# Angle inputs, low-rank gate product and weight unit 2 in the opening of a decoder-block kernel

## The chip, the cores and the metric

The kernel runs on one core of a Trainium2 chip. The metric is the device time of one execution in microseconds. A core has five engines with a queue each: TensorE (PE, matrix products), VectorE (DVE), ScalarE (ACT), GpSimd (POOL) and SyncE (SP), which here issues nearly all DMAs. Each engine runs its program in order; they meet through semaphores.

## What is computed

A decoder block on x of 256 tokens by 1024. Cut to what matters here:

```python
h = rms_norm(x, norm1_gain[l])
proj = h @ w_in[l]
gq, gk, gv, gr, g_low, mq, mk, mv = parts      # widths 256, 256, 512, 512, 16, 512, 512, 512
gate_logit = g_low @ w_gate_up[l] + b_gate[l]  # low rank: 16
log_a = jax.nn.log_sigmoid(gate_logit) / GLA_GATE_TAU
...                                            # gated linear attention on gq, gk, gv, log_a, gr
q_m = rotary(to_heads(mq, MOBA_HEADS), positions)   # ang = positions * inv_freq; cos, sin
k_m = rotary(to_heads(mk, MOBA_HEADS), positions)
...                                            # causal attention, both groups normed
x = x + jnp.concatenate([o_gla, o_moba], axis=-1) @ w_out[l]
h = rms_norm(x, norm2_gain[l])
x = x + (jax.nn.silu(h @ w_ffn_gate[l]) * (h @ w_ffn_up[l])) @ w_ffn_down[l]
return rms_norm(x, final_norm_gain)
```

## The kernel before

All is f32. A large product is made of three f32r products, `hi*hi + hi*lo + lo*hi`: for every weight, ScalarE casts it from `raw` to `w_hi`, and VectorE subtracts, `w_lo = raw - w_hi`; the activations (`aT_hi`, `aT_lo`) are split alike. Weights come as *units* of 128x2048 (1 MB) through three `raw` slots into rings of six for hi and lo. An in-projection unit is half the depth (four chunks of 128) of one block of 512 columns. Units 0 and 1 are special: they are loaded, cast and multiplied as eight *rows* of 128x512 (`load_first`, `split_first`, `first_row`), so that TensorE can begin early. `unit_ready(u)` is TensorE's wait for a unit, `raw_free(u)` SP's wait for a slot.

The order on every engine is written out by hand. TensorE's opening: 14 warm-up products of zeros, the eight transposes of x tile 0 into the PSUM banks `aux` 0 to 3 (chunks 2b and 2b+1 share bank b), three small transposes to bring the norm gains and the frequencies to partitions, two warm-ups, the transposes of x tile 1, two small transposes more (frequencies spread to 128 rows, positions to partitions), the eight rows (`first_row`), the low-rank product (`gate_low`), the transpose of the other gains (`other_gains`), then the units 2 to 11 (`in_unit`), with the attention's products between them; the logits (`logits`) stand in the middle of unit 2.

ScalarE's opening: `take_xT` scales two chunks of x's transpose by the gains out of PSUM into `aT_hi`, in turn with `split_first` of the rows 1 to 7; then the low weights' cast, `split(2)`, two sums of squares for the norm (`sum_squares`), `split(3)`, and `take_block(0)`. VectorE: the gains' copy, two small copies for the angles, row 0 (cast and low part), then per chunk the `aT_lo` and the row's low part; then the angle work (`pos_f`, `ang`, `nearest_turns`, `turns_hi`, `turns_lo`), unit 2's low part (`split(2)`, L1137), four subtractions of multiples of two pi (`take_off`), the copy of the low-rank result (`lowT`, L1199), the other gains, and so on.

The low-rank product before: the 16 columns of low weights stand in 128 stationary columns (four times a hi and a lo part of 16); sixteen f32r matmuls of 256 columns, `aT_hi` and `aT_lo` per chunk, add up in one place of `aux` bank 2; `w_up` has the up weights on the partitions 0 to 31 (hi and lo), zeros elsewhere.

## Time and profile before

| what | value |
|---|---|
| median of 3 runs | 302.25 us (301.93 to 302.3) |
| the profiled execution | 301.75 us |
| its span in the trace | 300.0 us |
| TensorE busy | 292.4 us, 97% of the span |
| VectorE, ScalarE, GpSimd busy | 242.4, 171.6, 19.1 us |
| granted TensorE clock, mean | 0.996 |

The profile is one execution. The span runs from the first to the last recorded instruction; the execution's own time has 1.75 us more around it. Rows name an instruction by engine, line, operation and tiles (written<-read). PE rows are matmuls, PEld the loads of their stationary operand. In the chain of waits each piece is what the next one waited for, so its pieces add up to the span; in a timeline instructions can overlap by their pipelines.

### The profile page before, as it was taken

The numbers are of one execution on the slowest core, as the hardware profiler recorded it, in microseconds if no ns is written. First come the engines' busy times: TensorE is split into PE (matmuls) and PEld (weight loads), VectorE is DVE, ScalarE is ACT, GpSimd is POOL, SyncE is SP. The second block draws the span as 40 slices with busy tenths as digits, with TensorE's granted clock in tenths as the row PEclk, the third lists the DMA queues.
The fourth block names the chain that finished last, engine by engine and source line by source line (L and its number), as shares of the span: only waits on it lengthen the run. The fifth ranks groups of instructions, "written<-read, shape, count | busy, mean of one in ns | idle before, by whom it ended". The sixth has DMA issues, their size and how long they took to land.

```text
span 300.0 us, 4026 instructions
## 1 busy us (share of the span) xinstructions
PE 292.4 (97%) x1373; PEld 243.3 (81%) x1373; DVE 242.4 (81%) x403; ACT 171.6 (57%) x242; POOL 19.1 (6%) x41
## 2 busy tenths in 40 slices
PE   7999999999999999999999999999999999999992
PEld 7788888788898888887888888888888888888881
DVE  1999999977879687988888888889897978787155
ACT  2898999969765897717170808080808080813123
POOL 5050100000021001300000000000000000000011
PEclk9999999999999999999999999999999999999998
DMA  7987836737867121392929292929291929030003
GB/s 235 364 289 266 263 119 251 218 131 264 298 190 227 53 92 70 95 329 90 331 82 336 79 343 69 346 66 352 63 363 47 367 54 366 25 120 0 0 0 140
DMA packets 37318, 55.45 MB, mean 185 GB/s; under 512 B 2950, under 2 KB 26554, under 8 KB 37306
## 3 DMA queue, kind: packets, MB, share of 16 engines
q1 hardware_dynamic: 37140, 55.13, 54.4%
q10 hardware_dynamic: 166, 0.17, 0.2%
q8 instruction: 7, 0.11, 0.2%
q14 instruction: 5, 0.04, 0.0%
HBM read 53.72 MB, written 1.57 MB: 184 GB/s over the span
## 4 chain that ended last, share of the span: by engine, by line
PE 94%; DMA 2%; DVE 1%; issue 1%; POOL 1%; ACT 0%; SPq 0%; POOLq 0%; DVEq 0%
PE acc L508 15%; PE acc L510 15%; PE acc L509 15%; PE aux L508 13%; PE aux L509 13%; PE aux L510 13%; DMA raw<-in_w_in 2%; PE aux L613 1%; PE acc L562 1%; PE acc L565 1%; PE acc L568 1%; PE aux L683 1%; DVE x_sb L1366 1%; PE aux L707 1%; PE aux L665 1%
## 5 line engine op out<-in xcount | busy, mean ns | idle before, releaser
L1137 DVE TENSOR_TENSOR w_lo<-raw,w_hi 128x2048 fp32r<-128x2048 f32 x47 | 105.6, 2286 | 14.5 <-ACT w_hi L877 14.4
L877 ACT CAST w_hi<-raw 128x2048 fp32r<-128x2048 f32 x47 | 87.9, 1908 | 4.4 <-DMA raw<-in_w_ffn_up 2.1
L508 PE MATMUL aux<-w_hi,aT_hi 128*128 128x512 f32 (+1 forms) x180 | 69.8, 388 | 0.0
L509 PE MATMUL aux<-w_lo,aT_hi 128*128 128x512 f32 (+1 forms) x180 | 69.7, 387 | 0.0
L510 PE MATMUL aux<-w_hi,aT_lo 128*128 128x512 f32 (+1 forms) x180 | 69.7, 387 | 0.0
L1432 DVE STREAM_TRANSPOSE reuse_c<-reuse_c 32x128 f32<-32x128 f32 x160 | 48.4, 303 | 2.4
L1080 ACT CAST pT_hi<-reuse_c 128x512 fp32r<-128x512 f32 x10 | 6.2, 621 | 72.9 <-DVE reuse_c L1432 72.9
L508 PE MATMUL acc<-w_hi,aT_hi 128*128 128x512 f32 x118 | 47.1, 399 | 0.0
L510 PE MATMUL acc<-w_hi,aT_lo 128*128 128x512 f32 x118 | 46.1, 390 | 0.0
L509 PE MATMUL acc<-w_lo,aT_hi 128*128 128x512 f32 x118 | 46.0, 390 | 0.0
L508 PEld LDWEIGHTS aux<-w_hi,aT_hi 128*128 128x128 f32 x180 | 33.8, 188 | 6.9
L510 PEld LDWEIGHTS aux<-w_hi,aT_lo 128*128 128x128 f32 x180 | 33.8, 188 | 6.9
L509 PEld LDWEIGHTS aux<-w_lo,aT_hi 128*128 128x128 f32 x180 | 33.8, 188 | 6.8
L508 PE MATMUL acc<-w_hi,pT_hi 128*128 128x512 f32 x80 | 31.3, 392 | 0.0
L510 PE MATMUL acc<-w_hi,pT_lo 128*128 128x512 f32 x80 | 31.2, 390 | 0.0
L509 PE MATMUL acc<-w_lo,pT_hi 128*128 128x512 f32 x80 | 31.2, 389 | 0.0
L510 PEld LDWEIGHTS acc<-w_hi,aT_lo 128*128 128x128 f32 x118 | 22.2, 188 | 4.8
L508 PEld LDWEIGHTS acc<-w_hi,aT_hi 128*128 128x128 f32 x118 | 22.2, 188 | 4.7 <-issue 0.2
L509 PEld LDWEIGHTS acc<-w_lo,aT_hi 128*128 128x128 f32 x118 | 22.2, 188 | 4.4
L1063 ACT ACTIVATE reuse_c<-aux,rstd 128x256 f32<-128x256 f32 x22 | 10.0, 471 | 19.1 <-PE aux L510 17.9
L508 PEld LDWEIGHTS acc<-w_hi,pT_hi 128*128 128x128 f32 x80 | 15.0, 188 | 3.4 <-issue 0.3
L510 PEld LDWEIGHTS acc<-w_hi,pT_lo 128*128 128x128 f32 x80 | 15.0, 188 | 3.2
(203 smaller groups left out, 285.0 us busy)
## 6 DMA issues: line engine op xcount, KB each, us to landing
raw<-in_w_ffn_gate SPq DMA_DIRECT2D x22, 512.0 KB, 4.3
raw<-in_w_ffn_up SPq DMA_DIRECT2D x22, 512.0 KB, 5.4
raw<-in_w_ffn_down SPq DMA_DIRECT2D x22, 512.0 KB, 6.0
raw<-in_w_in SPq DMA_DIRECT2D x20, 512.0 KB, 4.8
raw<-in_w_out SPq DMA_DIRECT2D x8, 512.0 KB, 4.3
raw<-in_w_in SPq DMA_DIRECT2D x8, 256.0 KB, 6.2
x_sb<-in_x SPq DMA_DIRECT2D x2, 512.0 KB, 3.7
m_moves<-reuse_c SPq DMA_DIRECT2D x1, 512.0 KB, 2.7
```

The costliest lines, as they stand in the source:

```text
L508: nc.tensor.matmul(dst, left_hi[:, k, tok], right_hi, start=first, stop=False)
L509: nc.tensor.matmul(dst, left_hi[:, k, tok], right_lo, start=False, stop=False)
L510: return nc.tensor.matmul(dst, left_lo[:, k, tok], right_hi, start=False, stop=last)
L562: nc.tensor.matmul(acc[:, t, :], aT_hi[:, k, toks[t]], right_hi, start=k == 0, stop=False)
L565: nc.tensor.matmul(acc[:, t, :], aT_hi[:, k, toks[t]], right_lo, start=False, stop=False)
L568: last = nc.tensor.matmul(acc[:, t, :], aT_lo[:, k, toks[t]], right_hi, start=False, stop=k == KC - 1)
L613: last = nc.tensor.transpose(aux[:, bank, n * P:(n + 1) * P], src, ident[:, :])
L877: nc.scalar.copy(w_hi[:, slot % RING, :], raw[:, slot % RAW, :]).then_inc(hi_ready, 1)
L1063: nc.scalar.activation(silu_g[:, t, :], aux[:, GATE_UP_BANKS[parity][t], 0:FF], ACT.Silu, scale=rstd[:, 1, t:t + 1]).then_inc(silu_ready, 1)
L1080: nc.scalar.copy(dst, src.rearrange("p (k s) -> p k s", k=2)).then_inc(hiddenT_hi_ready, 1)
L1137: nc.vector.tensor_tensor(w_lo[:, slot % RING, :], raw[:, slot % RAW, :], w_hi[:, slot % RING, :].bitcast(f32), ALU.subtract).then_inc(lo_ ...
L1432: last = nc.vector.transpose(cols[SQUARE * c:SQUARE * (c + 1), :, :, g, :], rows[SQUARE * g:SQUARE * (g + 1), :, :, c, :])
```

## The change

Six things change in the opening; from unit 3 on the order is the same.

1. Positions and frequencies are loaded to the partitions where they are used: positions as 256 single elements, frequencies as one row repeated to 128 partitions, first and second on ScalarE's queue. The three small transposes and two copies that did this go. The norm gains' DMA moves to SP, between the two x tiles.
2. SP issues weight row 0, waits for x tile 0, and then issues the rows 1 to 7.
3. VectorE's angle work up to `turns_lo` stands ahead of row 0 and around the gains' copy.
4. The low-rank product works in f32: POOL multiplies the raw low weights by the gains, ScalarE copies x's transposes unscaled out of PSUM (`copy_xT`, four copies of 128x512), and eight matmuls write four column groups of 32, two chunks to a group. The logits product adds the groups, `w_up` holding four copies.
5. Unit 2 is cast and split in two halves, each with a load semaphore of its own. The order of `lowT` and the subtractions changes.
6. `fill` counts the loads of a `raw` slot, of which unit 2 no longer uses the common semaphore; `take_block(0)` waits for the low-rank product, since its target shares memory with the copies.

```diff
+        low_w = reuse_d[:, 512:512 + KC * SQUARE].rearrange("p (k w n) -> p k w n", k=KC, n=RANK)
+        xT_raw = [half[:, :].rearrange("p (b n) -> p b n", b=2)[:, b, :] for half in (reuse_a, reuse_b) for b in range(2)]
...
             for t in range(T):
                 sp.dma_start(x_sb[:, t, :], x[0, t * P:(t + 1) * P, :]).then_inc(x_loaded[t], 16)
-            for n in range(KC):
+                if t == 0:
+                    sp.dma_start(gain_rows[0:KC, :], norm1_gain.rearrange("l (k p) -> (l k) p", p=P)).then_inc(norm1_loaded, 16)
+            load_first(0)
+            sp.wait_ge(x_loaded[0], 16)
+            for n in range(1, KC):
                 load_first(n)
...
-            for n in range(2):
-                sp.dma_start(w_up[n * RANK:(n + 1) * RANK, :], w_gate_up[0]).then_inc(up_loaded, 16)
+            for n in range(QUADS):
+                sp.dma_start(w_up[n * SQUARE:n * SQUARE + RANK, :], w_gate_up[0]).then_inc(up_loaded, 16)
...
-                pe.wait_ge(xT_hi_ready, KC)
-                pe.wait_ge(xT_lo_ready, KC)
+                pe.wait_ge(low_w_ready, 1)
+                pe.wait_ge(xT_raw_ready, KC // 2)
                 for k in range(KC):
-                    left = w_hi[:, RING - 1, k * P:(k + 1) * P]
-                    nc.tensor.matmul(aux[:, 2, 0:SEQ], left, aT_hi[:, k, :], start=k == 0, stop=False)
-                    last = nc.tensor.matmul(aux[:, 2, 0:SEQ], left, aT_lo[:, k, :], start=False, stop=k == KC - 1)
+                    group = slice(k % QUADS * SQUARE, (k % QUADS + 1) * SQUARE)
+                    last = nc.tensor.matmul(aux[group, 2, 0:SEQ], low_w[:, k, :, :].rearrange("p w n -> p (w n)"),
+                                            xT_raw[k // 2][:, k % 2 * SEQ:(k % 2 + 1) * SEQ], start=k < QUADS, stop=k >= QUADS)
...
-            act.dma_start(gain_rows[0:KC, :], norm1_gain.rearrange("l (k p) -> (l k) p", p=P)).then_inc(norm1_loaded, 16)
-            act.dma_start(freq_row, inv_freq).then_inc(freq_loaded, 16)
-            act.dma_start(pos_i, positions.rearrange("b (t p) -> (b t) p", p=P)).then_inc(pos_loaded, 16)
+            with nc.allow_non_contiguous_dma("one position a partition"):
+                act.dma_start(pos_i, positions.rearrange("b (t p) -> p (b t)", p=P)).then_inc(pos_loaded, 16)
+            act.dma_start(freq, inv_freq.to_broadcast([P, HALF])).then_inc(freq_loaded, 16)
```

VectorE at the start of the program, before, from its first instruction to row 0's low part (`reuse_c` holds the small inputs):

```order
L1161 MEMSET w_lo 128x256
L1163 COPY gains<-acc 128x8
L1166 COPY reuse_c<-acc 64x1
L1168 CAST reuse_c<-reuse_c 2x128
L1156 CAST w_hi<-raw 128x512
L1158 TENSOR_TENSOR w_lo<-raw,w_hi 128x512
```

The same place in the changed kernel (`reuse_e` holds angles and turns, `w_lo` the cast turns):

```order
L1162 MEMSET w_lo 128x256
L1171 CAST pos_f<-reuse_c 128x2
L1175 TENSOR_SCALAR reuse_e<-reuse_c,pos_f 128x64 x2
L1164 TENSOR_SCALAR reuse_e<-reuse_e 128x128
L1165 TENSOR_SCALAR reuse_e<-reuse_e 128x128
L1179 COPY gains<-acc 128x8
L1181 CAST w_lo<-reuse_e 128x128
L1182 TENSOR_TENSOR reuse_e<-reuse_e,w_lo 128x128
L1157 CAST w_hi<-raw 128x512
```

Five angle instructions (L1171 to L1165) now stand ahead of the gains' copy and two behind it, all ahead of row 0's cast.

ScalarE from the last chunks of x to unit 3, before:

```order
L900 ACTIVATE aT_hi<-aux,gains 128x256 x2
L906 CAST w_hi<-raw 128x512 x2
L916 CAST w_hi<-low_raw 128x32x16
L877 CAST w_hi<-raw 128x2048
L883 ACTIVATE reuse_f,ss<-x_sb 128x1024 x2
L877 CAST w_hi<-raw 128x2048
```

The same place in the changed kernel (`reuse_a` and `reuse_b` take the unscaled x):

```order
L892 ACTIVATE aT_hi<-aux,gains 128x256 x2
L905 COPY reuse_a<-aux 128x512
L898 CAST w_hi<-raw 128x512 x2
L905 COPY reuse_a<-aux 128x512
L916 CAST w_hi<-raw 128x1024 x2
L905 COPY reuse_b<-aux 128x512 x2
L875 ACTIVATE reuse_f,ss<-x_sb 128x1024 x2
L869 CAST w_hi<-raw 128x2048
```

The cast of the low weights is gone, four copies have come, and two of them stand behind unit 2's halves.

## Rows read from the trace of the kernel before

**Rows 1.** The page: busy time of the engines, and the chain's shares.

```profile
PE 292.4 (97%) x1373; PEld 243.3 (81%) x1373; DVE 242.4 (81%) x403; ACT 171.6 (57%) x242; POOL 19.1 (6%) x41
...
PE 94%; DMA 2%; DVE 1%; issue 1%; POOL 1%; ACT 0%; SPq 0%; POOLq 0%; DVEq 0%
```

**Rows 2.** Chain of waits, first 10 us: start, length, what.

```profile
0.80 0.38 SPq L336
...
1.71 5.34 DMA raw<-in_w_in
...
7.07 0.44 DVE w_hi L1156
...
7.64 0.70 PE acc L562 x2
...
9.01 0.47 PE acc L568 x2
```

**Rows 3.** Chain of waits, around the low-rank product (16 pieces, L589 and L590).

```profile
19.02 0.12 PE aux L589
...
20.82 0.12 PE aux L590
20.93 0.15 PE aux L577
21.09 0.43 PE acc L508
```

**Rows 4.** Chain of waits: f32 products (logits; attention output; state update).

```profile
24.04 0.86 PE aux L620 x4
...
76.99 1.45 PE aux L683 x13
78.44 0.59 PE aux L695 x8
```

**Rows 5.** Timeline of ScalarE, 12 to 16 us: start, length, instruction, [idle before, releaser].

```profile
12.04 0.86 ACT L900 ACTIVATE aT_hi<-aux,gains 128x256 fp32r<-128x256 f32 x2
12.76 1.16 ACT L906 CAST w_hi<-raw 128x512 fp32r<-128x512 f32 x2
...
15.52 1.91 ACT L877 CAST w_hi<-raw 128x2048 fp32r<-128x2048 f32 x1 [1.07 <-DMA raw<-in_w_in]
```

**Rows 6.** One line's instructions: ScalarE copies of 128x512 from PSUM, min/median/max ns.

```profile
L979 ACT COPY reuse_f<-aux x2: 585/588/591, 69.5 to 70.0; 128x512 f32<-128x512 f32 x2
```

**Rows 7.** DMA issues of the first 8 us: count, size of each, median us to landing.

```profile
x_sb<-in_x SPq DMA_DIRECT2D x2, 512.0 KB, 3.7
...
low_raw<-in_w_in SPq DMA_DIRECT2D x1, 64.0 KB, 6.4
```

**Rows 8.** Timeline of VectorE, 14 to 21 us.

```profile
14.89 1.54 DVE L1158 TENSOR_TENSOR w_lo<-raw,w_hi 128x512 fp32r<-128x512 f32 x1
...
16.61 0.47 DVE L1188 TENSOR_SCALAR reuse_e<-acc,pos_f 128x64 f32<-128x64 f32 x2
...
17.64 0.23 DVE L1191 CAST w_lo<-reuse_e 128x128 fp32r<-128x128 f32 x1
17.90 0.29 DVE L1192 TENSOR_TENSOR reuse_e<-reuse_e,w_lo 128x128 f32<-128x128 f32 x1
18.22 2.29 DVE L1137 TENSOR_TENSOR w_lo<-raw,w_hi 128x2048 fp32r<-128x2048 f32 x1
```

**Rows 9.** Timeline of all engines, first 7 us; ACTq rows are issues.

```profile
1.44 0.23 ACTq L867 DMA_DIRECT2D reuse_c<-in_inv_freq  x1
...
5.36 0.11 PEld L545 LDWEIGHTS acc<-ident,reuse_c 1*64 1x64 f32 x1
...
5.57 0.17 DVE L1163 COPY gains<-acc 128x8 f32<-128x8 f32 x1 [4.38 <-PE acc L542]
...
5.84 0.20 DVE L1168 CAST reuse_c<-reuse_c 2x128 f32<-2x128 int32 x1
6.31 0.84 ACT L900 ACTIVATE aT_hi<-aux,gains 128x256 fp32r<-128x256 f32 x2 [3.04 <-PE aux L534]
```

More of the change, by code:

```diff
@@ L349, in rows_unit @@
                                   w[row + h * half * P:row + (h + 1) * half * P, col:col + width]
-                                  .rearrange("(k p) n -> p k n", p=P)) for h in range(2)])
+                                  .rearrange("(k p) n -> p k n", p=P)) for h in range(2)], sems)
             def gate_up_unit(slot, j, h):
@@ L914, in _ @@
                     take_xT((n + 1, n + 2) if n < KC - 1 else ())
-            act.wait_ge(low_loaded, 16)
-            nc.scalar.copy(low_w[:, :, :, 0, :], low_raw[:, :, :].unsqueeze(2).to_broadcast(LOW_COPIES)).then_inc(low_hi_ready, 1)
-            split(2)
+                if n in (5, KC - 1):
+                    copy_xT((n - 5) // 2)
+            for h in range(2):
+                act.wait_ge(half_loaded[h], 16)
+                half = slice(h * UNIT // 2, (h + 1) * UNIT // 2)
+                nc.scalar.copy(w_hi[:, EARLY, half], raw[:, EARLY, half]).then_inc((half_hi_ready, hi_ready)[h], 1)
+            for pair in range(2, KC // 2):
+                copy_xT(pair)
             for t in range(T):
@@ L1161, in _, with nearest_turns, take_off @@
             nc.vector.memset(warm.bitcast(f32), 0.0).then_inc(warm_built, 1)
+            def nearest_turns():
+                then(nc.vector.tensor_scalar(turns, ang, 1.0 / (2.0 * np.pi), MAGIC, ALU.mult, ALU.add))
+                then(nc.vector.tensor_scalar(turns, turns, -MAGIC, None, ALU.add))
+            def take_off(n, part):
+                then(nc.vector.scalar_tensor_tensor(out=ang, in0=n, scalar=-part, in1=ang, op0=ALU.mult, op1=ALU.add))
+            dve.wait_ge(pos_loaded, 16)
+            nc.vector.tensor_copy(pos_f[:, :], pos_i).then_inc(pos_ready, 1)
+            dve.wait_ge(pos_ready, 1)
+            dve.wait_ge(freq_loaded, 16)
+            for t in range(T):
+                last = nc.vector.tensor_scalar(ang[:, t * HALF:(t + 1) * HALF], freq, pos_f[:, t:t + 1], None, ALU.mult)
+            then(last)
+            nearest_turns()
             dve.wait_ge(gains_in_psum, 1)
```

94 lines of the change are left out of this document (36 added, 58 removed).

## The prediction

> **What bounds the kernel now.** I read the page first: TensorE is busy for 292.4 of 300.0 us, and the chain that ended last is 94% TensorE [rows 1]. So a change pays only where TensorE waits or where it has less to do. Then I read the chain of waits at the two places that the diff touches. At the start the chain runs through the DMA of weight row 0 (issued at 1.71, landed after 5.34 us), VectorE's cast of that row at 7.07, and TensorE's first weight product at 7.64; the third group of products, at 9.01, follows without a hole [rows 2], and from there to the end of the eight rows TensorE is the chain. The second place is the end of the rows: sixteen low-rank products of 0.12 us each from 19.02 to 20.93, then the transpose of the other gains (0.15), and unit 2's first product at 21.09 [rows 3]. Nothing stands between them, so the 1.91 us of the low-rank product are on the path to the last instruction, and what is saved there comes off the whole, provided its new inputs and unit 2 are ready sooner too.
>
> **The low-rank product.** It becomes eight f32 matmuls with 256 moving columns and 32 result partitions, four column groups in turn. The trace shows one f32 matmul as two records: the two logits matmuls, also 256 columns, are four records in 0.86 us, 0.215 each [rows 4]. Sixteen records one behind the other would be 3.44 us. Whether groups run side by side is read from the state update L695: four f32 matmuls of 128 columns, in two column groups of 64, take 0.59 us for eight records, while whole-array matmuls of the same length, L683, take 1.45 for thirteen, 0.1115 each [rows 4]. Eight in a row would be 0.89. In pairs they are 4 x 0.1115 = 0.45, and 0.14 is left over for changing the array's form. So two groups do overlap. With four, sixteen records make four rounds: 4 x 0.215 + 0.14 = 1.00 us. The transpose behind it uses another form, so I charge the 0.14 once more: 1.14. No row shows four groups at once. The bounds are 1.00 (four, one change of form), 1.87 (only pairs: 8 x 0.215 + 0.14 = 1.86) and 3.44 (none); I take 1.14, since the nearest row, L695, has the full overlap that its number of groups allows. Term: 1.14 - 1.91 = **-0.77 us**, with -0.91 and +1.53 as its ends.
>
> The Trainium skill, "TensorE: Matmul & The Clock Gate", Part 3, gives a 2.38-fold speedup for three column tiles, 79% of the ideal; carried to four tiles, an estimate from that page, 3.44 / 3.17 = 1.09 us and a term of -0.82. Its page "TensorEngine Tiling (Array Packing)", Key Properties, says that a change of the tiling mode drains the engine; the 0.14 in L695 agrees.
>
> **What the product now waits for.** TensorE stands at the gate for the scaled weights from POOL and for four copies of the transposed x by ScalarE, and every later matmul is queued behind that wait. ScalarE, from its rows: the chunks 6 and 7 at 12.04 take 0.86 (to 12.90) [rows 5]; the first copy of 128x512 out of PSUM takes 0.59 [rows 6] (13.49), two casts 1.16 (14.65) [rows 5], the second copy 0.59 (15.24). Then unit 2 in halves: the whole cast took 1.91 and had waited for its DMA until 15.52, so both halves are there by 15.52, and the halves end near 16.2 and 17.2. Two more copies: 18.4. TensorE arrives at 19.02, so 0.6 us are spare. If the halves land later by more than that, TensorE waits for the excess. The cast of the low weights leaves ScalarE, which paid for part of the copies. POOL's one operation has half as many elements as the one before and no longer waits for ScalarE; the weights' DMA is issued later on SP but has 6.4 us to landing mostly because of the queue ahead of it [rows 7], which stays the same.
>
> **Unit 2 and VectorE.** Before, the angle steps from 16.61 to 18.22 stood ahead of unit 2's low part, which ran from 18.22 to 20.51 [rows 8], 0.58 ahead of TensorE. Now these steps have moved ahead of row 0, and after the last row (14.89 + 1.54 = 16.43) only two subtractions of 0.32 (spacing as of 17.90 to 18.22) stand before the two halves, 2.29 together: ready at about 19.4. TensorE needs it at 19.02 + 1.14 + 0.15 = 20.3. So the shorter product is not caught by unit 2; without the moved angle work it would have been (20.51 against 20.3). That cover is what the angle move is worth: it gives no time of its own. ScalarE's squares and unit 3 come about 1 us later (18.4 against 15.52 + 1.91 = 17.43 before [rows 5]); I cost that at nothing, since TensorE's share of the chain leaves no room for a wait on the units from 3 on [rows 1], and unit 3 is wanted only after all of unit 2.
>
> **The start.** VectorE now waits for positions and frequencies before it copies the norm gains, and behind that copy are ScalarE's first chunk, VectorE's row 0 and all of TensorE. Its work from the landing F of the frequencies to the cast of row 0: from 16.61 to 17.64 for products and turns (1.03), the gains copy 0.17 [rows 9], then 17.64 to 18.22 for the split of the turns (0.58) [rows 8]: 1.78. Row 0 stands at 7.07, so the work is hidden if F is below 5.29. Before, the frequency row was second on ScalarE's queue (issued at 1.44) and TensorE took it at 5.36, behind other work; positions, third, were taken at 5.84 without a wait for them [rows 9]. Both are upper bounds. The x tiles, 512 KB each, needed 3.7 us from issue [rows 7]; from 1.44 that is F = 5.14, and a small load is hardly slower than a tile. So I take no shift. The loads are more pieces than before, 256 single positions and 128 rows of frequencies, and may push row 0 by some tenths. In the other direction, the seven rows that SP now holds back until x tile 0 has landed (by 0.80 + 3.7 = 4.5) are not in row 0's way; the earliest TensorE could start is with the first chunk, 6.31 + 0.42 = 6.73 instead of 7.64 [rows 2, 9]. Bounds of the start: -0.9 and, without the rival below, +0.5; taken 0. Held-back row 1, issued at 4.5 and landed after 3.7 like a tile in an empty queue, is there at 8.2; its cast takes 0.58 and TensorE wants it at 9.01 + 0.47 = 9.48. Behind the held rows on SP are the low weights, unit 2, the gains, four copies of the up weights (two issues more) and unit 3; the queue of transfers is full throughout, so I cost these at nothing. The small transposes taken off TensorE lie in its wait for row 0 and are worth nothing.
>
> **Sum.** 301.75 us was the profiled execution (span 300.0); 301.75 - 0.77 = 300.98 there. The median of the runs is 302.25, 0.5 above it; on that footing 302.25 - 0.77 = **301.5 us**. A measurement of this kernel can tell about 0.2%, 0.6 us, from no change, so faster means under 301.65.
>
> **Rivals.** (1) *Only pairs overlap.* The product then takes 1.86 and the gain is 0.05: 302.2 us. For it: the trace shows two groups and no more. Against: L695 uses all of its groups. (2) *No overlap with 32-wide groups*, so the change does not do what it says: 3.44, thus +1.53: 303.8 us. Against: both L695's time and its form. (3) *The angle inputs come late*, the one on the slower side: VectorE is stopped at its first instruction of the program's real work, and gains, row 0 and TensorE with it. If the frequencies land like the low weights, which also come in small pieces, after 6.4 us [rows 7], F is 1.44 + 6.4 = 7.84, row 0 is cast at 9.62 instead of 7.07, +2.55, and the whole is +1.78: 304.0 us. It costs from F = 5.29, eats the gain at 6.06 and shows as slower from about 6.66. Between, with F at 5.84 as the positions' bound, +0.55 leaves -0.22: 302.0. For it: the pieces are small and share the engines with 1 MB of x; against: they are issued first. The Trainium skill, "DMA: Bandwidth & Descriptors", Rules for kernel authors, says that a non-contiguous last dimension becomes one descriptor per element, and to rearrange it; no row here shows that price. (4) *The copies come late*: unit 2's halves land 0.6 us or more after 15.5, TensorE waits at the gate, and up to the whole 0.77 is given back: about 302.1.
>
> **How the numbers follow.** Forecast (four groups overlap, inputs in time) 0.50; pairs only 0.18; angle inputs mildly late (302.0) 0.14; copies late 0.06; angle inputs clearly late (304.0) 0.07; no overlap 0.05. Faster by over 0.2%: 0.50. Within: 0.18 + 0.14 + 0.06 = 0.38. Slower: 0.12. The forecast's own range is 301.0 to 301.9 (its ends for the change of form, and a few tenths of the start). The range reaches up over pairs-only and the mild delay with some spread of the runs, to 302.6, and leaves out the 0.12 of the slower cases; down to 300.9, with half of the start's lower bound.
>
> **What would show it.** In the changed trace: the eight products' chain at 1.0 to 1.2 us (pairs: 1.9; none: 3.4); no idle TensorE ahead of them, and unit 2's halves done before the transpose of the gains; row 0's cast still waiting for its DMA near 7.1, not for the angle steps. The prediction is wrong if TensorE's first weight product is over 0.3 us later than 7.64 or if the gate waits for ScalarE.

## The result, and the profile after

The changed kernel takes 302.86 us (median of 13 runs, 301.94 to 303.72), the kernel before 302.17 in the same job: a ratio of 1.0029, 95% interval 1.0020 to 1.0038. It is slower by about 0.7 us; the forecast was 301.5, its range ended at 302.6. One TensorE job became shorter by more than was forecast, and all of it, and more, was lost elsewhere. The page of the changed kernel, busy time and the chain's shares, beside [rows 1]:

```profile
PE 291.7 (97%) x1370; PEld 241.3 (80%) x1370; DVE 241.9 (80%) x402; ACT 172.8 (57%) x246; POOL 16.7 (6%) x41
...
PE 78%; DVE 6%; DMA 4%; ACT 4%; issue 3%; SPq 3%; POOL 1%; POOLq 0%; DVEq 0%
```

TensorE works 0.7 us less, and yet the span is 1.4 us longer (301.4 against 300.0). The two profiled executions took 303.08 and 301.75, so this pair differs by 1.3 us where the medians differ by 0.7. Its share of the chain fell from 94% to 78%: the chain that ended last now leaves TensorE for a long stretch. The changed kernel's chain of waits from 18 to 60 us shows where:

```profile
14.25 7.86 DMA raw<-in_w_in
...
22.13 1.92 ACT w_hi L869
...
24.14 0.09 DVE w_lo L1138
...
53.59 0.70 DVE reuse_e L1243
...
54.34 1.09 PE aux L605 x8
```

Read it from the top: unit 3's load lands at 22.1, ScalarE casts it, VectorE subtracts, and from there the chain stays with VectorE and ScalarE until the rotary embedding (`rotate`, L1243 ends it), for whose result TensorE's transposes at 54.34 wait. In the kernel before the same stretch was TensorE's alone; its chain at the rotation:

```profile
53.08 0.98 PE aux L613 x8
```

Now the place of the product, in the timeline of TensorE, changed kernel:

```profile
19.34 0.61 PE L562 MATMUL acc<-w_hi,aT_lo 128*128 128x512 f32 x2
19.89 0.64 PE L581 MATMUL aux<-reuse_a,reuse_d 128*32 128x256 f32 x8
20.34 0.61 PE L581 MATMUL aux<-reuse_b,reuse_d 128*32 128x256 f32 x8
20.89 0.23 PE L571 MATMUL aux<-ident,reuse_d 10*128 10x10 f32 x1
21.05 0.50 PE L509 MATMUL acc<-w_hi,aT_hi 128*128 128x512 f32 x1
```

Sixteen records in 1.00 us (19.89 to 20.89), and unit 2 follows without a stall. The same view of the kernel before, from the last row's end to unit 2:

```profile
18.41 0.62 PE L568 MATMUL acc<-w_hi,aT_lo 128*128 128x512 f32 x2
18.86 0.28 PE L589 MATMUL aux<-aT_hi,w_hi 128*128 128x256 f32 x1
...
21.02 0.50 PE L508 MATMUL acc<-w_hi,aT_hi 128*128 128x512 f32 x1
```

There the product begins 0.45 us after the row's last pair and takes 21.02 - 18.86 = 2.16 us to unit 2. Now it begins 0.55 after that pair, so a hole of 0.10 stands ahead of it, and 21.05 - 19.89 = 1.16 lie behind its start: 1.26 instead of 2.16. The product gave 0.90 us. But the start had lost as much. The changed kernel's timeline of VectorE and TensorE, first 9 us ([idle before, releaser]):

```profile
5.25 0.17 DVE L1171 CAST pos_f<-reuse_c 128x2 f32<-128x2 int32 x1 [4.06 <-DMA reuse_c<-in_positions]
6.04 0.42 DVE L1175 TENSOR_SCALAR reuse_e<-reuse_c,pos_f 128x64 f32<-128x64 f32 x2 [0.62 <-DMA reuse_c<-in_inv_freq]
7.31 1.09 PE L535 MATMUL aux<-ident,x_sb 128*128 128x128 f32 x8 [0.71 <-DMA x_sb<-in_x]
8.57 0.70 PE L556 MATMUL acc<-w_hi,aT_hi 128*128 128x512 f32 x2 [0.17 <-DVE w_hi L1157]
```

The frequencies were there at 6.04, not at 5.14; x tile 1 was waited for until 7.31; the first weight product came at 8.57, against 7.64 [rows 2]. So TensorE reached unit 2 level with before (+0.93 - 0.90 = +0.03, 21.05 against 21.02). The second loss is a wait that TensorE did not have before. Waits of VectorE and of TensorE, changed kernel (sum, times, longest):

```profile
DVE w_lo L1138 <- ACT w_hi L869: 1.4, 1, 1.4
DVE lowT L1199 <- PE aux L581: 1.2, 1, 1.2
...
PE aux L605 <- DVE reuse_e L1243: 1.2, 1, 1.2
```

VectorE waits 1.2 for the low-rank product and then 1.4 for unit 3's cast, and 30 us later TensorE waits 1.2 for VectorE. The same two views of the kernel before, from 7 to 56 us (VectorE) and from 19 to 58 (weight loads):

```profile
DVE w_hi L1156 <- DMA raw<-in_w_in: 1.0, 1, 1.0
DVE reuse_c L1245 <- ACT reuse_c L934: 0.3, 1, 0.3
...
PEld aux L613 <- DVE reuse_e L1240: 0.3, 1, 0.3
```

The prediction never asked how long VectorE's own chain is. From row 0 to the rotation VectorE of the kernel before waits once, 0.3 us in 45; and TensorE's weight load L613 already waits for the rotation. VectorE was a second chain of the same length as TensorE's, hidden behind a 94%.

### The profile page after: what moved, and what is told of

Read it like the earlier page. It is cut to its first block, busy times and chain, and to the rows that moved or that the text cites. A ratio compares the mean times of both kernels' runs of the same rounds, so it can differ in the third digit from the quotient of the medians.

```text
span 301.4 us, 4019 instructions
## 1 busy us (share of the span) xinstructions
PE 291.7 (97%) x1370; PEld 241.3 (80%) x1370; DVE 241.9 (80%) x402; ACT 172.8 (57%) x246; POOL 16.7 (6%) x41
## 4 chain that ended last, share of the span: by engine, by line
PE 78%; DVE 6%; DMA 4%; ACT 4%; issue 3%; SPq 3%; POOL 1%; POOLq 0%; DVEq 0%
PE aux L509 13%; PE aux L511 13%; PE aux L510 13%; PE acc L509 11%; PE acc L511 11%; PE acc L510 11%; DMA raw<-in_w_in 3%; PE aux L605 2%; ACT w_hi L869 1%; DMA x_sb<-in_x 1%; SPq L328 1%; DVE w_lo L1138 1%; PE aux L675 1%; DVE x_sb L1369 1%; SPq L342 1%
## 5 line engine op out<-in xcount | busy, mean ns | idle before, releaser
L1138 DVE TENSOR_TENSOR w_lo<-raw,w_hi 128x2048 fp32r<-128x2048 f32 x46 | 103.3, 2286 | 16.2 <-ACT w_hi L869 16.1
L869 ACT CAST w_hi<-raw 128x2048 fp32r<-128x2048 f32 x46 | 85.9, 1908 | 5.0 <-DMA raw<-in_w_ffn_up 2.5
```

The costliest lines, as they stand in the source:

```text
L869: nc.scalar.copy(w_hi[:, slot % RING, :], raw[:, slot % RAW, :]).then_inc(hi_ready, 1)
L1138: nc.vector.tensor_tensor(w_lo[:, slot % RING, :], raw[:, slot % RAW, :], w_hi[:, slot % RING, :].bitcast(f32), ALU.subtract).then_inc(lo_ ...
```

## Experiments

On record in the prediction is theory T: TensorE alone sets the end, what happens from unit 3 on on other engines is free. Theory V came from the two lists of waits above: VectorE has no slack from row 0 to the rotation in the kernel before, and the end follows whichever of the two chains is later there. The kernel before took 302.0 to 302.2 in every job, and ratios are to it in the same job.

**A. What makes the start late.** First without SP's wait for x tile 0:

```diff
             load_first(0)
-            sp.wait_ge(x_loaded[0], 16)
             for n in range(1, KC):
                 load_first(n)
```

> The changed kernel without SP's wait for x tile 0: the weight rows 1 to 7 are issued right behind row 0. Theory 'hold' (SP's queue is late, so unit 3 lands late and VectorE with it): SP reaches unit 3's first issue at about 11.8 to 12.6 us instead of 13.78, ScalarE casts unit 3 near 20 instead of 22.13, the wait of TensorE for the rotation at 54 us shrinks from 1.2 us to under 0.4, and the time is 0.8 to 1.3 us under the changed kernel's. Theory 'pieces' (the single positions and frequency rows slow everything from the start): the first product stays near 8.6, unit 3 stays late by at least 1 us, gain under 0.4 us.

Measured 303.46, ratio 1.0044 (1.0028 to 1.0060): 0.6 above the changed kernel, which neither theory expected. Its profile is of the fastest of its six executions (302.48), so what made the others slower stays open. In it TensorE has x tile 1 at 8.05 instead of 7.31 and the first product is at 9.34: the wait is no loss at the start. Unit 3 was issued at 13.86, as late as with the wait (13.78), so the wait by itself does not set that issue either. But unit 3 was in time there (cast at 21.14 without a wait), and there was no stall at the rotation. Next, the positions as two rows, with the angles worked out from zeros:

```diff
-                act.dma_start(pos_i, positions.rearrange("b (t p) -> p (b t)", p=P)).then_inc(pos_loaded, 16)
+            act.dma_start(reuse_c[0:T, 2 * P:3 * P].bitcast(i32), positions.rearrange("b (t p) -> (b t) p", p=P)).then_inc(pos_loaded, 16)
...
+            then(nc.vector.memset(reuse_c[:, 0:T], 0.0))
```

> The changed kernel with the positions loaded as two rows of 128 to a place that nobody reads; the angles are computed from zeros, so the rotation is left out of the result. All waits stay. Theory 'pieces': x tile 0 lands 0.5 us or more sooner than 4.81, x tile 1 1 us or more sooner than about 7.2, the first weight product is at 7.6 to 7.9 instead of 8.57, and as SP's wait ends sooner, unit 3 comes 0.7 to 1 us sooner: 0.8 to 1.3 us under the changed kernel. Theory 'hold': x tile 0 and the first product move by 0.3 us at most, and so does the time.

Measured 302.70, ratio 1.0026 (1.0015 to 1.0038): hardly better. The reverse, the kernel before with an unused load of the 256 single positions:

```diff
+                act.dma_start(extra[:, :], positions.rearrange("b (t p) -> p (b t)", p=P)).then_inc(extra_loaded, 16)
             act.dma_start(gain_rows[0:KC, :], norm1_gain.rearrange("l (k p) -> (l k) p", p=P)).then_inc(norm1_loaded, 16)
```

> The kernel before with one more load, first on ScalarE's queue: the positions as 256 single elements to a place that nobody reads; no one waits for it. The price of the pieces by itself. Theory 'pieces': x tile 1 and row 0 land 0.6 to 1 us later, the first product is at 8.2 to 8.6 instead of 7.64, and the time is 0.5 to 1 us over the kernel before. If the pieces cost nothing: within 0.2 us.

Measured 302.46, ratio 1.0038 (1.0013 to 1.0064; two of twelve executions at 305.8 and 306.0 draw it up, the median is 0.14% above). And the kernel before with SP's wait added:

```diff
-            for n in range(KC):
+            load_first(0)
+            sp.wait_ge(x_loaded[0], 16)
+            for n in range(1, KC):
                 load_first(n)
```

> The kernel before with SP's wait for x tile 0 ahead of the rows 1 to 7, nothing else. Theory 'hold': row 0 as before, unit 3's first issue at about 12.8 to 13.3 instead of 11.84; if that alone makes unit 3 late, ScalarE waits for it and the time is 0.5 us or more over the kernel before. Theory 'pieces': unit 3 has room for this delay (it was issued 7.6 us ahead of its cast), time within 0.3 us of before.

Measured 302.14, ratio 1.0004 (0.9991 to 1.0017): the wait alone costs nothing there. Then both loads cheap, the angles again worked out from zeros:

```diff
-                act.dma_start(pos_i, positions.rearrange("b (t p) -> p (b t)", p=P)).then_inc(pos_loaded, 16)
-            act.dma_start(freq, inv_freq.to_broadcast([P, HALF])).then_inc(freq_loaded, 16)
+            act.dma_start(reuse_c[0:T, 2 * P:3 * P].bitcast(i32), positions.rearrange("b (t p) -> (b t) p", p=P)).then_inc(pos_loaded, 16)
+            act.dma_start(reuse_c[0:1, 3 * P:3 * P + HALF], inv_freq).then_inc(freq_loaded, 16)
```

> The changed kernel with the two angle loads made cheap: positions come as two rows of 128 and the frequencies as one row, into memory that nothing reads; the angles are computed from zeros by the same instructions in the same places. So the angle values are not the reference's; all else is. If the many small pieces (256 single positions and 128 repeated frequency rows) are what delays the x tiles: x tile 1 lands by 5 us, the first weight product is at 7.0 to 7.7 instead of 8.6, and the time falls by 0.6 to 0.9 for the start, and by more if unit 3 is in time too, to 301.3 to 302.2. If the hold of SP or the angle work ahead of row 0 is what delays it, the first product stays at 8.3 or later and the time at 302.7 to 303.0.

Measured 302.51, ratio 1.0015 (0.9998 to 1.0032). The start is repaired: first product at 7.57. The stretch from 4 to 5 us shows by what; windows of the changed kernel, of the run with cheap positions only, and of the run with both loads cheap (busy times, granted clock, busy share of the DMA engines, GB/s):

```profile
4.00:5.00 1.00, 0.61 (x4) 0.38 (x4) 0.00 (x0) 0.00 (x0) 0.87 (x6) 1.00 0.37 85
```

```profile
4.00:5.00 1.00, 1.00 (x9) 1.00 (x9) 0.00 (x0) 0.00 (x0) 0.87 (x6) 1.00 0.18 56
```

```profile
4.00:5.00 1.00, 1.00 (x9) 0.85 (x9) 0.50 (x3) 0.00 (x0) 0.87 (x6) 1.00 0.82 295
```

The transfers stand at 85 and 56 GB/s while x is to come, with the DMA engines mostly idle, and run at 295 without the two loads. The frequencies alone (one row of 256 bytes read 128 times) do it. But the time fell by 0.35 only, since with the start repaired unit 3 was still late. The same run's waits:

```profile
DVE w_lo L1137 <- ACT w_hi L868: 2.3, 1, 2.3
...
PE aux L605 <- DVE reuse_e L1243: 1.5, 1, 1.5
```

**B. The second chain.** The direct test of V adds one VectorE instruction to the kernel before:

```diff
+            nc.vector.tensor_tensor(extra[:, :], x_sb[:, 0, 0:768], x_sb[:, 1, 0:768], ALU.add)
             split(3)
```

> The kernel before with one instruction more: VectorE adds two pieces of x, 128x768, into memory that nothing reads, ahead of unit 3's low part; about 1.0 us by the rate of its 128x512 operations (0.69). No result depends on it. Theory V: VectorE has no slack to the rotation, which comes 0.8 to 1.0 us later, and so does the end: about 302.9 to 303.1. Theory T: TensorE is the chain and does not wait for VectorE; the time stays at 302.1 to 302.2.

Measured 303.04, ratio 1.0031 (1.0019 to 1.0042). The instruction (timeline) and the new wait (waits of TensorE) in that run:

```profile
23.33 0.96 DVE L1205 TENSOR_TENSOR extra<-x_sb 128x768 f32<-128x768 f32 x1
```

```profile
PE aux L614 <- DVE reuse_e L1242: 0.7, 1, 0.7
```

0.96 us of VectorE work cost 0.93 at the end (303.04 - 302.11): T falls, V holds. The start of this execution was late, 8.60 in the table below; the profile of the kernel before with SP's wait, with a start as late (8.53), has the rotation's last operation at 52.90, this one at 53.86, again 0.96 apart. Then the changed kernel with its start undone (angle inputs, angle work and loads as before; the new product and unit 2 in halves stay):

```diff
+            act.dma_start(freq_row, inv_freq).then_inc(freq_loaded, 16)
+            act.dma_start(pos_i, positions.rearrange("b (t p) -> (b t) p", p=P)).then_inc(pos_loaded, 16)
...
+            nearest_turns()
+            then(nc.vector.tensor_copy(turns_hi, turns))
+            then(nc.vector.tensor_tensor(turns_lo, turns, turns_hi.bitcast(f32), ALU.subtract))
             for h in range(2):
                 dve.wait_ge((half_hi_ready, hi_ready)[h], 1)
```

> The changed kernel with its start undone: angle inputs loaded as three short rows and spread by TensorE, rows 1 to 7 not held back, angle work behind the last row, as before the change; the low-rank product in four column groups and unit 2 in halves stay. Theory T (TensorE alone sets the end, the start cost the gain): first weight product at 7.6 to 8.0 us, unit 2's first product about 0.8 us earlier than before, and the end 0.8 earlier too: about 301.3 us. Theory V (VectorE, which works without a gap from row 0 to the rotation at 52 us, sets the end there): VectorE's work is as long as before and starts as early, so the rotation comes when it came before, TensorE waits there for most of the 0.8 us it has gained, and the time is 301.9 to 302.2, within 0.1% of before.

Measured 302.27, ratio 1.0008 (0.9996 to 1.0021): the new product alone gives nothing. TensorE's unit 2 (timeline) and its wait at the rotation (waits) in that run:

```profile
20.59 0.50 PE L512 MATMUL acc<-w_hi,aT_hi 128*128 128x512 f32 x1
```

```profile
PE aux L615 <- DVE reuse_e L1256: 0.7, 1, 0.7
```

TensorE is at unit 2 0.4 us earlier than before (21.02 in the same view), though its first product was 0.49 later (8.13), and returns it at the rotation. VectorE still has the angle work behind the last row in this run; without moving it, the new product gives nothing. Last, the changed kernel with unit 3's load ahead of the small loads on SP:

```diff
+            in_units(RAW, RAW + 1)
             for row, n_rows, src in ((NORM2_ROW, KC, norm2_gain.rearrange("l (k p) -> (l k) p", p=P)),
...
-            in_units(RAW, 11)
+            in_units(RAW + 1, 11)
```

> The changed kernel with one thing moved: unit 3's load is issued on SP ahead of the loads of the other gains, the four copies of the up weights and the bias. Theory V: unit 3's cast no longer comes late, VectorE starts unit 3's low part at about 22.8 instead of 24.1 us (in a run with the same start), the wait of 1.2 us before the rotation's transposes goes, and the time falls by about 1 us, from 302.9 to about 301.8 to 302.0. Theory T: nothing that happens at unit 3 counts; the time stays at 302.9.

Measured 302.12, ratio 1.0006 (0.9994 to 1.0017): 0.74 us below the changed kernel, and no wait of TensorE at the rotation beyond the old 0.3 of the weight load. The late unit 3 is the loss that the changed kernel shows. Two profiles with the same start say it most directly. The last kernel of part D has its first product at 8.58 and unit 2 at 21.05, the changed kernel at 8.57 and 21.05; but there unit 3's low part starts at 22.74, not at 24.14, and the span is 300.0, not 301.4:

```profile
22.74 2.29 DVE L1149 TENSOR_TENSOR w_lo<-raw,w_hi 128x2048 fp32r<-128x2048 f32 x1
```

One table gathers the profiles of A and B: from each, TensorE's first weight product, VectorE's start of unit 3's low part, the start of the rotation's last operation, and the span.

| kernel | first product | unit 3's low part | rotation's last | span | span less rotation |
|---|---|---|---|---|---|
| before | 7.64 | 22.79 | 52.22 | 300.0 | 247.8 |
| after | 8.57 | 24.14 | 53.59 | 301.4 | 247.8 |
| after, no hold | 9.34 | 23.51 | 52.98 | 300.7 | 247.7 |
| after, cheap loads | 7.57 | 24.04 | 53.48 | 301.3 | 247.8 |
| before + VectorE's 0.96 | 8.60 | 24.21 | 53.86 | 301.7 | 247.8 |
| new product only | 8.13 | 22.94 | 52.63 | 300.4 | 247.8 |
| after, unit 3 early | 9.34 | 24.01 | 53.48 | 301.2 | 247.7 |

The span is the rotation's last start plus 247.7 to 247.8, and the rotation comes 29.4 to 29.7 after unit 3's low part. The first product, from 7.57 to 9.34, does not order the spans where unit 3 is late. Where unit 3 is in time, it does. VectorE waits for the low-rank product before it copies `lowT`; in the run with unit 3 early:

```profile
DVE lowT L1201 <- PE aux L583: 2.5, 1, 2.5
```

In all nine profiles that have the angle work moved, whole or in part, and unit 3 in time (no hold, position rows and unit 3 early above, six more below), unit 3's low part starts 1.70 to 1.71 us after that copy. So VectorE has slack ahead of the copy and none behind it, and a late start reaches the end through the product. This fits that unit 3 early brings the time back to 302.1 and not below: the start's +0.93 stands against the product's -0.90.

**C. Why unit 3 is late.** The changed kernel once more, unaltered:

> The changed kernel once more, unaltered, on the same chip as the two beside it and with a second profile. Theory V: 302.6 to 303.0; in the profile the start of VectorE's low part of unit 3 and the rotation are 29.4 to 29.7 us apart whatever the first product's time is, and if unit 3's cast is late again, TensorE waits at the rotation. If the wait at the rotation was chance in the first profile, it is absent here and the end follows the first product.

Measured 302.99 (8 runs), ratio 1.0038 (1.0024 to 1.0052); first product 9.15, unit 3's cast waits 1.75 us for its load until 22.31, TensorE 1.0 at the rotation, span 301.7 with the rotation at 53.92. So it is no chance of one profile. SP's issues, changed kernel:

```profile
11.57 1.70 SPq L377 DMA_DIRECT2D w_up<-in_w_gate_up  x4
13.31 0.42 SPq L378 DMA_DIRECT2D mv<-in_b_gate  x1
13.78 13.57 SPq L342 DMA_DIRECT2D raw<-in_w_in  x8
```

Unit 3 is the first of the last row, issued at 13.78 (before: 11.84). And after the bias (`mv<-in_b_gate`, one row of 1 KB read 128 times) the transfers collapse for 3 us. Two runs tell how the late issue and this hole add up. The first changes only the source of the bias:

```diff
-            sp.dma_start(gate_bias, b_gate.to_broadcast([P, QK])).then_inc(bias_loaded, 16)
+            sp.dma_start(gate_bias, w_in[0, 0:P, 0:QK]).then_inc(bias_loaded, 16)
```

> The changed kernel with another source for the gate bias: 128 different rows of the in-projection's weights (1 KB each) instead of one row of 1 KB read 128 times; size, target and place on SP are the same, the values are not the reference's. In the changed kernel's trace the transfers fall to about 100 to 260 GB/s for some 2 us while the bias and the up weights are in flight, just ahead of unit 3, with single packets of 2 KB taking up to 1.8 us. If reading one address over and over causes that hole: it goes, unit 3's cast comes at about 20.5 instead of 22.1 to 22.3, TensorE no longer waits 1.0 to 1.2 at the rotation, and the time is 302.0 to 302.4. If not: the hole stays and the time is 302.7 to 303.0.

Measured 302.13, ratio 0.9997 (0.9988 to 1.0006). Windows of the changed kernel, then of this run:

```profile
15.00:16.00 1.00, 1.00 (x6) 0.81 (x5) 1.00 (x3) 1.00 (x2) 0.00 (x0) 1.00 1.29 263
16.00:17.00 1.00, 1.00 (x6) 0.84 (x5) 1.00 (x3) 0.94 (x2) 0.00 (x0) 1.00 0.65 108
17.00:18.00 1.00, 1.00 (x7) 0.81 (x6) 0.93 (x3) 1.00 (x3) 0.00 (x0) 1.00 0.80 260
```

```profile
15.00:16.00 1.00, 1.00 (x6) 0.84 (x5) 0.83 (x2) 1.00 (x3) 0.30 (x1) 1.00 1.05 367
16.00:17.00 1.00, 1.00 (x6) 0.81 (x5) 1.00 (x4) 1.00 (x2) 0.00 (x0) 1.00 1.09 270
17.00:18.00 1.00, 1.00 (x6) 0.84 (x5) 0.93 (x4) 0.86 (x2) 0.00 (x0) 1.00 1.06 347
```

In these 3 us the changed kernel moves 0.63 MB, the same loads with 128 different rows 0.98. The bias was issued at 14.13 here, 0.8 later, but the next microsecond shows no hole either (373). Unit 3, issued at 14.60, later still, was in time: its cast starts at 21.46 behind ScalarE's own work, with no wait for the load. The second run leaves out two of the four copies of the up weights, and with them half of the logits' sum:

```diff
-            for n in range(QUADS):
+            for n in range(2):
                 sp.dma_start(w_up[n * SQUARE:n * SQUARE + RANK, :], w_gate_up[0]).then_inc(up_loaded, 16)
```

> The changed kernel with two of the four copies of the up weights left out (the logits then lack half of their sum). SP comes to unit 3's load 0.85 us earlier and 32 rows of 1 KB fewer are moved. If it is SP's later issue and these copies that make unit 3 late: its cast starts at 21.2 or earlier, the wait at the rotation shrinks to 0 to 0.4, time 302.0 to 302.5. If unit 3's transfer is slow for another reason: the cast stays at 22 and the time at 302.7 to 303.0.

Measured 302.32, ratio 0.9998 (0.9987 to 1.0009); unit 3's cast at 20.57, no wait. The same three windows of this run:

```profile
15.00:16.00 1.00, 1.00 (x6) 0.84 (x5) 1.00 (x3) 1.00 (x3) 0.00 (x0) 1.00 1.11 276
16.00:17.00 1.00, 1.00 (x6) 0.81 (x6) 1.00 (x3) 1.00 (x2) 0.00 (x0) 1.00 1.02 358
17.00:18.00 1.00, 1.00 (x6) 0.84 (x5) 0.93 (x4) 1.00 (x2) 0.00 (x0) 1.00 1.05 389
```

That is 1.02 MB: the hole is gone here too, though the bias is still one row read 128 times. The kernel before, also with two copies, moves 383, 384 and 317 GB/s from 12 to 15 us, behind its bias at 11.38. So the repeated row does not make the hole alone; the two copies more have a part in it, and this run does not test the later issue by itself. What the issue does is an estimate from the traces. The second half of unit 3 was issued at 14.25 and landed after 7.86 us, at 22.11; before it was issued at 12.31 and took 6.2, with different rows 5.5, with two copies 5.9. ScalarE was free for it at 20.6. The later issue with the transfer of before gives 14.25 + 6.2 = 20.4, the old issue with the slow transfer 12.31 + 7.86 = 20.2: either alone would have been in time, and unit 3 is late by some 1.5 us through both. Both cures at once were not run.

**D. Can the saved 0.9 us reach the end?** Positions and frequencies now come as one row each, and TensorE makes the angles (a product with one stationary row); unit 3 stands early:

```diff
+            for t in range(T):
+                last = nc.tensor.matmul(ang_psum[:, t * HALF:(t + 1) * HALF], pos_row[:, t * P:(t + 1) * P], freq,
+                                        start=True, stop=True)
```

> The changed kernel with both delays taken away and the full computation: positions and frequencies come as one row each, TensorE multiplies them (two f32 products with one stationary row) into PSUM, VectorE's angle work stays ahead of row 0 and after it; unit 3's load is issued ahead of the small loads. Theory V (the end is the later of TensorE's chain and VectorE's, which runs without a gap from unit 3's low part for 29.45 us to the rotation): first weight product at 7.5 to 8.2, unit 2's first product 0.4 to 0.95 us earlier than before, VectorE starts unit 3's low part at 21.7 to 22.3 instead of 22.79, no wait at the rotation beyond the old 0.3; time 301.2 to 301.7. Theory T (the start alone): the same start gives 301.3 as well, but then the run with cheap loads alone, 302.5, remains unexplained. If a third thing holds unit 3 back (its transfer is slow wherever it is issued): VectorE waits for it by over 1 us and the time is 302.2 to 302.8.

Measured 302.09, ratio 1.0008 (0.9992 to 1.0024): a miss. The run's VectorE:

```profile
6.64 0.17 DVE L1183 COPY gains<-acc 128x8 f32<-128x8 f32 x1 [3.31 <-PE acc L554]
6.84 0.29 DVE L1174 TENSOR_SCALAR reuse_e<-acc 128x128 f32<-128x128 f32 x1
...
8.02 0.43 DVE L1167 CAST w_hi<-raw 128x512 fp32r<-128x512 f32 x1
```

My own placing has a part in it: four turn instructions between the gains' copy and row 0, which waits for them until 8.02. But row 0 had landed only at 7.78 (issued at 2.06, 5.7 us), so they cost 0.24 us of the start. The same without SP's wait for x tile 0:

```diff
-            sp.wait_ge(x_loaded[0], 16)
```

> The kernel of the run beside it (angles as a product on TensorE, unit 3 early) without SP's wait for x tile 0, so that all eight rows are issued at once. If the hold only helps the x tiles and row 0: the start is later by 0 to 0.5 us and the time is 301.3 to 302.0, not below the run beside it. If the hold makes unit 3 late even with its issue moved up: VectorE starts unit 3's low part earlier by 0.3 or more and the time is lower than the run beside it.

Measured 302.56, ratio 1.0007 (0.9993 to 1.0021), not better. The kernel before with only these early angles:

```diff
+            nearest_turns(ang_psum)
+            then(nc.vector.tensor_copy(turns_hi, turns))
+            then(nc.vector.tensor_tensor(turns_lo, turns, turns_hi.bitcast(f32), ALU.subtract))
             split_first(0)
```

> The kernel before with the angle work alone made shorter and moved ahead of row 0 (positions and frequencies as one row each, their product on TensorE); its low-rank product, order of loads and undivided unit 2 stay. VectorE reaches unit 3's low part up to 1.8 us earlier. Theory V: VectorE's chain no longer matters, but TensorE's is as long as before, so the time stays within 0.3 of before: 301.8 to 302.2. Together with the run that had the new low-rank product alone (no gain) and the run with both, this tells whether each of the two parts is worth nothing without the other. Against V: a gain of 0.6 or more here would mean that VectorE alone sets the end before.

Measured 302.74, ratio 1.0021 (1.0009 to 1.0033): slower, against my expectation. The same placing holds back row 0's cast there, to 8.80; but in this profile TensorE has no wait ahead of its first product at 9.45, so that the placing is the cause is not shown. Early angles as built there are a loss by themselves, and this run doesn't tell what free ones would be worth. Then the turns behind the last row:

```diff
-            nearest_turns(ang_psum)
...
             split_first(0)
...
+            nearest_turns(ang_psum)
+            then(nc.vector.tensor_copy(turns_hi, turns))
```

> The kernel with the angles as a product on TensorE, the held rows and the early unit 3, with one thing moved: VectorE's turns (four instructions, 1.2 us) stand behind the last row instead of between the gains' copy and row 0, where the profile showed them to delay row 0's cast from about 7.0 to 8.0. The full computation. Theory V: the first weight product comes at 7.4 to 7.9 in an execution whose first transposes run at the full rate, unit 2's first product about 0.7 us earlier than before; VectorE still reaches the low-rank result before TensorE has it, so unit 3's low part starts at 21.8 to 22.3 instead of 22.79, and the end is 0.5 to 0.9 earlier: 301.3 to 301.7. Rival (ScalarE and the loads are as tight as VectorE from unit 3 on): unit 3's or 4's cast comes late, VectorE or TensorE waits for it, and the time stays at 301.9 to 302.2.

Measured 301.73, ratio 0.9999 (0.9983 to 1.0016); its executions fall into a group from 300.9 to 301.9 and one from 302.4 to 303.2. The profile is of the second group (302.44), and there the rival named in the expectation stands:

```profile
24.52 1.91 ACT L879 CAST w_hi<-raw 128x2048 fp32r<-128x2048 f32 x1 [1.15 <-DMA raw<-in_w_in]
...
29.70 0.69 DVE L1226 SCALAR_TENSOR_TENSOR reuse_b<-reuse_b 128x512 f32<-128x512 f32 x1 [0.80 <-ACT reuse_b L938]
```

Unit 4's load is late by 1.15 us, ScalarE's softplus stands behind its cast, VectorE waits 0.80, TensorE 1.0 at the rotation. The same without SP's wait:

```diff
-            sp.wait_ge(x_loaded[0], 16)
```

> The run beside it without SP's wait for x tile 0. If the hold is what brings x and row 0 early: first weight product 0.2 to 0.6 later, time 0.1 to 0.5 above the run beside it. If the hold is what delays the units from 3 on: time below it by 0.2 or more. Against the run with the new low-rank product alone (302.3, no gain) the only differences are VectorE's work, shorter by about 0.9 us by the product on TensorE, and unit 3's place on SP: theory V gives 301.4 to 301.9.

Measured 301.92, ratio 1.0003 (0.9990 to 1.0017). Last, the up weights and the bias behind unit 4's load as well:

```diff
+            in_units(RAW + 1, RAW + 2)
+            sp.wait_ge(up_zeroed, 1)
+            for n in range(QUADS):
+                sp.dma_start(w_up[n * SQUARE:n * SQUARE + RANK, :], w_gate_up[0]).then_inc(up_loaded, 16)
+            sp.dma_start(gate_bias, b_gate.to_broadcast([P, QK])).then_inc(bias_loaded, 16)
+            in_units(RAW + 2, 11)
```

> The kernel with the angles as a product on TensorE, the turns behind the rows and unit 3 early, with the up weights' copies and the bias moved on SP behind unit 4's load as well. The full computation. There unit 4's cast waited 1.15 us for its load and VectorE 0.8 for what stands behind that cast. If these small loads ahead of unit 4 cause it: no such wait, TensorE's 0.4 to 0.9 us from unit 2 reach the end, 301.2 to 301.6. If the small loads now come late themselves: TensorE or VectorE waits at the logits (needed at about 24), and the time is 302 or more.

Measured 301.56, ratio 0.9982 (0.9967 to 0.9998). The same kernel again:

> The run with the small loads behind unit 4 once more, unaltered, for a second interval against the kernel before. If its gain is real: 301.3 to 301.8, ratio 0.997 to 0.9985. If it was chance: 302.0 to 302.3. In the profile the span is the start of the rotation's last operation plus 247.8 us, as in every kernel so far.

Measured 301.74, ratio 0.9997 (0.9986 to 1.0008), a smaller gain than the ratio that I expected. In its profile VectorE's rotation and TensorE's first product:

```profile
8.09 0.69 PE L568 MATMUL acc<-w_hi,aT_hi 128*128 128x512 f32 x2 [0.21 <-DVE w_hi L1168]
...
51.85 0.69 DVE L1249 TENSOR_TENSOR reuse_e<-reuse_e,mv 128x512 f32<-128x512 f32 x1
```

Rotation at 51.85 and span 299.6, 0.4 below before, though the first product is 0.45 later. Over both jobs (24 runs) its median is 301.69, that of before 302.17 (46 runs): 0.5 us by the medians, 0.3 by the means (301.82 and 302.12), but of the two intervals one reaches above 1, so a gain over the kernel before is likely and not shown. It is well below the changed kernel (302.95, 21 runs).

So the product's 0.9 us does reach the end, and the start takes it back. In three profiles of this part no late load stops VectorE behind the product: no hold with the turns behind the rows, the last kernel, and its repetition. Their first products are at 8.61, 8.58 and 8.09, their spans 300.0, 300.0 and 299.6. The span before plus the delay of the first product over 7.64 less 0.90 gives 300.1, 300.0 and 299.6. No run here has both a start at 7.64 and unit 3 in time.

## Why the prediction was wrong, point by point

- **The low-rank product: right, a little small.** Taken -0.77, measured -0.90. Four groups run side by side: sixteen records in 1.00 us, four rounds of 0.225 and a hole of 0.10 behind them, and another 0.10 ahead. So both changes of form are there, at 0.10 instead of 0.14, and the new product came out at 1.10 for the 1.14 taken. The rest is the old product, taken as 1.91: in the timeline it took 2.00 to the transpose of the gains, with 0.08 of a hole there too. The estimate from the Trainium skill, "TensorE: Matmul & The Clock Gate", Part 3 (2.38-fold for three column tiles) was 1.09 for the records; 3.44 / 1.00 is 3.4-fold for four.
- **The gate and unit 2: right.** No idle TensorE ahead of the product, unit 2's halves done before it; VectorE waits 1.2 us for the product.
- **The start: wrong.** The failed step is "a small load is hardly slower than a tile". The frequencies were used at 6.04 and 6.81 in two profiles, not before 5.29, and x tile 1 was late too, which no term had. The first product was +0.93 and +1.50 late, past the 0.3 that the prediction named as a sign of being wrong. The rival with late angle inputs had the place right, and its rule (late by what the landing exceeds 5.29) gives +0.75 and +1.52, between its mild case of +0.55 and its clear one of +2.55; but it made the angle work the cause; with x itself held up, both were. The rule quoted there from the Trainium skill, "DMA: Bandwidth & Descriptors", Rules for kernel authors, on non-contiguous last dimensions, is borne out: the single positions added to the kernel before bring the packets of ScalarE's queue from 166 to 438. As for the price, the stretch from 4 to 5 us moved 176 GB/s instead of 296. The repeated frequency row, to which that rule doesn't apply, was the worse of the two.
- **"TensorE's share of the chain leaves no room for a wait on the units from 3 on": wrong, and the step that decides.** A share of 94% says which chain ended last, not how far behind the next one is. VectorE was level with it: 0.96 us more work on it cost 0.93. The prediction priced unit 3's delay on ScalarE "at nothing" by this step.
- **The angle move, "no time of its own": right, but for too small a reason.** Alone it was slower (302.74). The prediction saw it as cover for unit 2, 20.51 against 20.3; without it the new product gave nothing (302.27), and TensorE waited 0.7 us at the rotation, which the prediction did not name.
- **SP's queue "at nothing": wrong.** A later issue (14.25 for 12.31, of which the two copies more are 0.92) and the hole behind the copies and the repeated row made unit 3's cast 1.5 us late. This accounts for the +0.7 of the median: each of three ways of undoing it brings 302.1 to 302.3.
- **The sum by profile:** +0.93 at the start, -0.90 by the product, +1.34 between unit 2 and the rotation, so +1.37; the span is 1.4 longer. Either loss hides a part of the other: with the start repaired and unit 3 still late the time fell by 0.35 only, and with unit 3 in time the start takes back what the product gave.
- **The rival on the slower side** was the angle inputs. The mechanism that made it slower, a weight unit late on VectorE's chain, wasn't among the rivals.

What stays open: whether the frequencies' repeated row acts through the same thing as the bias's (different rows were tried for the bias alone, and there the copies had a part), and what sets the later issue of unit 3 beside the two copies.

One thing more moves the start from one execution to the next, TensorE's clock. In the run with the positions as two rows, the eight transposes of both x tiles:

```profile
4.37 1.04 PE L535 MATMUL aux<-ident,x_sb 128*128 128x128 f32 x8
...
7.98 1.97 PE L535 MATMUL aux<-ident,x_sb 128*128 128x128 f32 x8 [1.99 <-DMA x_sb<-in_x]
```

and a window of the second, with the granted clock third from the right (the same run's window from 4 to 5 stands in A):

```profile
9.00:10.00 1.00, 1.00 (x6) 1.00 (x5) 0.97 (x3) 1.00 (x3) 0.00 (x0) 0.50 1.04 399
```

At 1.00 (the 2.4 GHz level) the transposes take 1.04 us, at 0.50 (1.2 GHz) 1.97; the clock fell while TensorE stood idle for x tile 1, from 5.99 to 7.98. The column does not always tell: in the trace the entries of the clock begin at 4.40 us in the changed kernel's profile and at 10.89 in that with unit 3 early, and where there is none the column reads 1.00. In all twenty profiles the transposes ahead of the first entry, or at a recorded 0.50, follow each other by 0.21 to 0.27 us, and those at a recorded 1.00 by 0.11 to 0.17. With the changed kernel's opening, the first product came at 8.57 and 9.15 where all transposes were fast and at 9.24 to 9.34 where some were slow. So the start is read from several profiles and from medians, not from one.

## What to carry to other kernels

Before a wait off the critical engine is called free, take the engine that feeds it and list its waits up to the next meeting point: if it waits nowhere, it is a second chain, and shortening the first one buys nothing until the second is shorter too. Look also for the place where the two meet on the way (here the low-rank product's copy): behind it, a delay of either is a delay of both. For every small load that is added or moved, look at what is in flight beside it and at who stands behind it on the issuing queue; "at nothing" and "hardly slower than a tile" missed it here. And a part that gives nothing alone may be the condition for another part: test them apart and together.

## What the runs showed of the hardware

One row read 128 times into 128 partitions can be a dear load. The bias (128 KB from 1 KB), behind four copies of the up weights, was followed by 3 us in which 0.63 MB moved, instead of 0.98 with different rows and 1.02 with two copies; and the frequencies (32 KB from 256 bytes) stood beside x at 56 GB/s. Four column groups of 32 in f32 overlapped fully: four rounds of about 0.22 us after each other (19.89 and 20.34 are two rounds apart), with holes of 0.10 ahead and behind.
